# Windowed attention of a hybrid encoder step: three loop turns replaced by one unrolled pipeline of 36 items of two heads

## The chip, the core and the metric

The kernel runs on one core of a Trainium2 chip. The metric is the device time of one execution, in microseconds (us); lower is better. The core has engines that run in parallel and wait for each other through semaphores: PE (TensorE, matrix products and transposes; its weight loads are listed apart as PEld), DVE (VectorE), ACT (ScalarE), POOL (GpSimd), and SP, whose queue issues transfers. SBUF is the on-chip memory and PSUM the eight banks that PE writes to.

## The reference, cut to what matters

Two layers of an encoder, for a prompt of 512 tokens and a sample of 64. Only the windowed attention of layer 0 is touched by the change: 24 query heads of width 64, three key/value heads (8 query heads share one), chunks of 64 queries that see 192 keys, a linear distance bias and a sink per head.

```python
s = jnp.einsum('bcqkgd,bcskd->bckgqs', qb, kb).astype(jnp.float32) / math.sqrt(HEAD_DIM)
bias = -alibi_slopes()[:, :, None, None] * jnp.abs(dist).astype(jnp.float32)
s = jnp.where(valid, s + bias[None, None], -jnp.inf)
# sink_probs:
m = jnp.maximum(jnp.max(scores, axis=-1, keepdims=True), sink)
p = jnp.exp(scores - m)
p = p / (jnp.sum(p, axis=-1, keepdims=True) + jnp.exp(sink - m))
o = jnp.einsum('bckgqs,bcskd->bcqkgd', p.astype(v.dtype), vb)
```

The sample's 64 queries do the same over 128 cached keys and their own 64. Before this stand the projections of queries, keys and values; behind it a cross attention into 256 memory tokens, the output projection, a feed-forward block, and then the second layer.

## The kernel before

All data are fp32. A projection is a product of a weight slab (128 output channels, 1024 inputs) with all 576 tokens. Each fp32 operand is split in a high and a low part, so that a slab takes eight **eighths** of six matmuls each (`eighth`, L841: w_hi with hi, w_lo with hi, w_hi with lo, each in two halves of 288 tokens). ACT splits off `w_hi` (L440), POOL computes `w_lo` (L1788), SP loads the next slab.

The attention is worked through in 12 **query tiles** of two heads each (128 channels), four tiles (`QT`) for each key/value head. A tile has five **units** (`UNITS_J`): unit 0 is the sample's part of both heads; units 1 and 2 are the first head's two halves of the prompt, units 3 and 4 the second head's. A half with the prompt's start ("small") has 128 + 256 score columns and three 128x128 blocks; the other ("big") has 256 + 256 and four. Each unit goes through a chain over three engines:

- **S** (`scores`, L920 and L929): PE writes scores into one of two PSUM banks;
- **B** (`bias_max`, L1392 and L1399): DVE adds the bias into `prob` (four buffers) and takes the maximum;
- **E** (`exps`, L548 to L555): ACT takes the exponential, its sums and the sink's term;
- **N** (`norm`, L1407 to L1413): DVE adds, takes the reciprocal and scales `prob`;
- **T** (`transposes`, L941 to L946): PE transposes the blocks into bank 6;
- **C** (`copy_t`, L566 to L570): ACT copies them to `p_t` (two buffers);
- **V** (`values`, L959, L960, L967): PE multiplies with the values into bank 7; after units 0 and 4 DVE copies the result out (**O**, L1293).

The order of these steps is a list written by `attention_steps`, and every engine takes its own steps from the list, in that order: S of unit t stands beside T of unit t-3 and V of unit t-4 (`LAG_T`, `LAG_PV`). Between them stand 32 eighths (**K**) of projections for later query tiles, four slabs per turn. When a slab's eighths are done, DVE turns the result into the next query tile (**Q**, `query_tile`, L1365 and L1367) and ACT splits the slab after next. The list holds 20 units, and each engine runs it three times in a loop over the key/value heads (`Fori(0, KVH)`). At the start of a turn DVE copies that head's keys, values and sinks to `k_cur`, `v_s`, `v_cur` and `sink_cur`, and PE's first S waits for that (`cur_ready`). Because semaphore values in a loop depend on the turn, engines compute them in registers. `alone` puts the waits ahead of B on an instruction of their own.

## Time and profile before

| | |
|---|---|
| time, median of 3 executions | 1993.61 us (1992.95 to 1995.2) |
| span of the profiled execution | 1990.5 us (the median lies 3.1 us above it) |
| PE busy | 1862.8 us, 94% |
| DVE busy | 844.8 us, 42% |
| ACT busy | 634.1 us, 32% |
| POOL busy | 844.5 us, 42% |
| DMA | 145.16 MB, mean 73 GB/s |

The span runs from the first instruction of the program to the last. A timeline row gives a start, a duration, the engine and line, and how many records were merged in it (x6). PE's records overlap, since matmuls are pipelined: what one group costs PE is the difference between its start and the start of the next group. An fp32 matmul of the attention has two records, one for each pass; a transpose has one. "Chain" is the work followed back from the end: what released what. PEclk is the granted clock of TensorE, 1.00 for 2.4 GHz and 0.50 for 1.2 GHz.

### The profile page before, as it was taken

What the parts mean: (1) busy time and instruction counts of PE and PEld (TensorE: products, weight loads), DVE (VectorE), ACT (ScalarE), POOL (GpSimd) and SP (SyncE); (2) the same over time, 40 slices, a digit from 0 to 9 for tenths busy, and PEclk for the clock granted to TensorE, in tenths of its full rate; (3) what the DMA queues carried; (4) which work ended last, traced back from release to release, by engine and by line L of the source; (5) the groups of instructions that cost most, each with busy time, mean ns of one, the idle gap of its engine ahead of it and who ended that gap; (6) DMA issues with size and microseconds to landing.
All of it is one profiled execution on the core that took longest, in us unless ns stands there. A gap on an engine that the chain in (4) does not pass through costs nothing.

```text
span 1990.5 us, 33561 instructions
## 1 busy us (share of the span) xinstructions
PE 1862.8 (94%) x13089; PEld 1746.9 (88%) x13089; DVE 844.8 (42%) x1609; ACT 634.1 (32%) x1118; POOL 844.5 (42%) x510
## 2 busy tenths in 40 slices
PE   6999999898999999997998989899898899999995
PEld 6987777798899999996997878787798899999995
DVE  6346666612511111125867686764711611111124
ACT  6225545522312221223333324242622312222121
POOL 1221111134645444445456464746134644444453
PEclk9999999999899999997999999999999799999997
DMA  6521111022122222221221212121022122222221
GB/s 207 185 80 48 32 47 47 28 85 74 54 82 78 84 84 84 75 84 54 65 64 41 75 42 65 42 72 55 30 85 84 43 85 78 82 84 84 81 78 69
DMA packets 42161, 145.16 MB, mean 73 GB/s; under 512 B 4832, under 2 KB 6496, under 8 KB 41824
## 3 DMA queue, kind: packets, MB, share of 16 engines
q1 hardware_dynamic: 40288, 140.07, 23.3%
q10 hardware_dynamic: 1792, 3.97, 0.5%
q8 instruction: 56, 0.92, 0.2%
q14 instruction: 25, 0.20, 0.0%
HBM read 137.61 MB, written 6.41 MB: 72 GB/s over the span
## 4 chain that ended last, share of the span: by engine, by line
PE 80%; DVE 10%; issue 4%; ACT 3%; POOL 2%; DMA 0%; DVEq 0%; ACTq 0%; SPq 0%; POOLq 0%
PE ps L841 66%; PE ps L929 2%; PE ps L967 2%; DVE u L1617 2%; DVE mix L1300 2%; PE ps L946 1%; DVE mix L1264 1%; PE ps L1163 1%; PE ps L1029 1%; PE ps L1006 1%; DVE big_lo L1247 1%; PE ps L812 1%; POOL x L1807 1%; DVE mix L1744 1%; PE ps L1215 1%
## 5 line engine op out<-in xcount | busy, mean ns | idle before, releaser
L1788 POOL TENSOR_TENSOR w_lo<-raw,w_hi 128x1024 fp32r<-128x1024 f32 x228 | 562.3, 2466 | 1026.5 <-ACT w_hi L440 1023.9
L841 PE MATMUL ps<-big_hi,w_hi 128*128 128x288 f32 x3616 | 804.4, 304 | 22.8 <-ACT big_hi L464 15.8
L841 PE MATMUL ps<-big_lo,w_hi 128*128 128x288 f32 x3616 | 786.9, 300 | 13.3 <-DVE big_lo L1247 13.1
L841 PE MATMUL ps<-big_hi,w_lo 128*128 128x288 f32 x3616 | 785.1, 299 | 0.0
L841 PEld LDWEIGHTS ps<-big_hi,w_hi 128*128 128x128 f32 x3616 | 590.0, 191 | 37.2 <-issue 30.8
L841 PEld LDWEIGHTS ps<-big_lo,w_hi 128*128 128x128 f32 x3616 | 590.4, 191 | 20.8 <-DVE big_lo L1247 20.6
L841 PEld LDWEIGHTS ps<-big_hi,w_lo 128*128 128x128 f32 x3616 | 592.2, 191 | 0.0
L440 ACT ACTIVATE w_hi<-raw 128x1024 fp32r<-128x1024 f32 x242 | 256.3, 1059 | 799.2 <-PE ps L841 782.1
L1539 DVE TENSOR_TENSOR mix<-ps,mix 128x576 f32<-128x576 f32 x64 | 48.4, 757 | 315.9 <-PE ps L841 315.9
L1527 DVE SCALAR_TENSOR_TENSOR relu<-ps,rstd 128x576 f32<-128x576 f32 x64 | 48.5, 757 | 311.6 <-PE ps L841 305.6
L1617 DVE SCALAR_TENSOR_TENSOR u<-xp,cpar,u 128x579 f32<-128x579 f32 x84 | 88.0, 1047 | 6.8 <-ACT u L703 4.8
L1282 DVE TENSOR_TENSOR sq_sum<-sq_sum,sq 128x576 f32<-128x576 f32 x24 | 19.9, 828 | 136.8 <-ACT sq L453 136.7
L1823 POOL TENSOR_TENSOR hid<-relu 128x576 f32<-128x576 f32 x64 | 73.5, 1148 | 8.5 <-DVE relu L1527 8.5
L1807 POOL TENSOR_TENSOR x<-x,mix 128x576 f32<-128x576 f32 x29 | 55.3, 1920 | 34.2 <-DVE mix L1300 18.0
L1392 DVE CUSTOM_DVE_ANT_0 prob<-ps,bias,sink_cur 128x128 f32<-128x128 f32 (+2 forms) x120 | 49.4, 442 | 37.1 <-PE ps L929 35.1
L548 ACT ACTIVATE prob<-prob,stat 128x256 f32<-128x256 f32 (+2 forms) x108 | 50.9, 472 | 41.6 <-DVE stat L1399 40.8
L1245 DVE TENSOR_TENSOR big_lo<-hid,big_hi 128x576 fp32r<-128x576 f32 x64 | 48.1, 751 | 28.4 <-POOL hid L1823 28.4
L1293 DVE TENSOR_SCALAR mix<-ps 64x64 f32 (+5 forms) x72 | 35.8, 497 | 52.5 <-PE ps L967 29.2
L841 PE MATMUL ps<-m_hi,w_hi 128*128 128x256 f32 x128 | 39.0, 305 | 15.4 <-POOL w_lo L1788 11.4
L759 ACT ACTIVATE dec<-ps 128x384 f32<-128x384 f32 (+1 forms) x40 | 16.1, 454 | 107.9 <-PE ps L1163 107.9
L929 PE MATMUL ps<-k_cur,q_t 64*128 64x128 f32 (+1 forms) x192 | 49.5, 378 | 0.0
L1707 DVE TENSOR_TENSOR dec<-dec,cbm 128x768 f32<-128x768 f32 (+1 forms) x20 | 26.7, 1337 | 48.3 <-ACT dec L759 48.3
(190 smaller groups left out, 1760.7 us busy)
## 6 DMA issues: line engine op xcount, KB each, us to landing
raw<-in_slabs SPq DMA_DIRECT2D x242, 512.0 KB, 3.6
bias<-in_alibi SPq DMA_DIRECT2D x14, 256.0 KB, 2.6
x<-in_x SPq DMA_DIRECT2D x2, 1152.0 KB, 6.6
out_y<-x SPq DMA_DIRECT2D x3, 576.0 KB, 2.8
out_h<-state ACTq DMA_DIRECT2D x4, 384.0 KB, 2.4
out_mv<-vm ACTq DMA_DIRECT2D x2, 512.0 KB, 5.8
kms<-in_mk SPq DMA_DIRECT2D x2, 512.0 KB, 5.4
vms<-in_mv SPq DMA_DIRECT2D x2, 512.0 KB, 7.0
```

The source lines that it names most:

```text
L440: act.activation(w_hi[:, s % 2], raw[:, s % 2], ACT.Copy).then_inc(hi_done, 1)
L548: act.activation(ap, ap, ACT.Exp, bias=stat[:, r, 1, b:b + 1], accum_out=stat[:, r, 2, b:b + 1])
L841: ins = pe.matmul(ps[:, 2 * (g % 2) + h, 0:hi_c - lo_c], w[:, s % 2, kt], a[:, k0 + kt, lo_c:hi_c], start=(start and kt == 0 and w is w_hi ...
L929: ins = pe.matmul(ps[:, bank, b * 2 * P + c:(b + 1) * 2 * P], q_t[e * HD:(e + 1) * HD, j, DEC + i * P:DEC + (i + 1) * P], k_cur[e * HD:(e ...
L1245: ins = dve.tensor_tensor(dst, src, hi.bitcast(F32), ALU.subtract)
L1392: ins = dve.tensor_tensor_reduce(prob[half, r, k, c0:c1], ps[half, bank, k * 2 * P + c0:k * 2 * P + c1], bias[half, j % 2, e, c0 + d:c1 + ...
L1527: dve.scalar_tensor_tensor(out=halves(relu[:, m % 2]), in0=src, scalar=0.0, in1=halves(rstd[:, 1]), op0=ALU.max, op1=ALU.mult).then_inc(fr ...
L1539: dve.tensor_tensor(halves(mix[:, m]), src, halves(mix[:, m]), ALU.add).then_inc(freed, 1)
L1617: dve.scalar_tensor_tensor(out=u[:, t], in0=xp[:, t % 2, j:j + UC], scalar=cpar[:, t, j:j + 1], in1=u[:, t], op0=ALU.mult, op1=ALU.add).th ...
L1788: pool.tensor_tensor(w_lo[:, s % 2], raw[:, s % 2], w_hi[:, s % 2].bitcast(F32), ALU.subtract).then_inc(lo_done, 1)
L1807: pool.tensor_tensor(x[:, m], x[:, m], mix[:, m], ALU.add).then_inc(x_done, 1)
L1823: pool.tensor_tensor(hid[:, m % 2], relu[:, m % 2], relu[:, m % 2], ALU.mult).then_inc(hid_done, 1)
```

## The change

The three turns become one straight list without a loop, over all 60 units, and with it go the copies to `k_cur`, `v_s`, `v_cur` and `sink_cur` (the products read `k_all`, `v_all` and `par`), the register arithmetic and `alone`. Units are renumbered: 1 and 2 are now the small halves of both heads, 3 and 4 the big ones. PE works in 36 **items** (`WORKS`), three for each tile: the sample, the two small halves, the two big halves. `scores` of a pair alternates matmul by matmul between the heads, that is between rows 0 to 63 and 64 to 127 of the array and between the two score banks. `values` of a pair alternates between columns 0 to 63 and 64 to 127, in one bank. The sample's values are four matmuls of 64 columns in place of two of 128, and one copy takes them out in place of two.

The list has 38 slots. Slot w holds S of item w, B of its units, V of item w-2, eighths, and then for each unit in turn E of item w and N and T of item w-1, with eighths between; O comes last. The 96 eighths are spread evenly, two or three in a slot.

```diff
+def work_units(w):
+    t = w // 3 * UNITS_J
+    return (t,) if w % 3 == 0 else (t + 2 * (w % 3) - 1, t + 2 * (w % 3))
 def attention_steps():
-    steps, k, total = [], 0, UNITS + LAG_PV
-    for t in range(total):
-        if t < UNITS:
-            steps.append(("S", t))
-        if 0 <= t - LAG_T < UNITS:
-            steps.append(("T", t - LAG_T))
-        while k < QT * KT and (k - 1) * (total - 1) <= t * QT * KT and k + 1 < KT * (1 + (t + 1) // UNITS_J):
-            steps.append(("K", k))
-            k += 1
-        if 0 <= t - LAG_PV < UNITS:
-            steps.append(("V", t - LAG_PV))
+    for w in range(slots):
+        goal = TILES * KT * (w + 1) // slots
+        new = work_units(w) if w < WORKS else ()
+        old = work_units(w - 1) if 0 <= w - 1 < WORKS else ()
+        if new:
+            steps.append(("S", w))
+        steps += [("B", t) for t in new]
+        if w >= 2:
+            steps.append(("V", w - 2))
+        fill(goal - 1 if len(old) > 1 else goal)
+        for c in range(2):
+            steps += [("E", t) for t in new[c:c + 1]]
+            steps += [(kind, t) for t in old[c:c + 1] for kind in "NT"]
+            if c < len(old):
+                fill(goal)
+        if w >= 2:
+            steps.append(("O", w - 2))
...
+                pe.wait_ge(biased, n_)
+                for b in range(2):
...
+                    for e in range(2):
+                        ins = pe.matmul(ps[:, S_BANK + (t + e) % 2, b * 2 * P + c:(b + 1) * 2 * P],
                                         q_t[e * HD:(e + 1) * HD, j, DEC + i * P:DEC + (i + 1) * P],
-                                        k_cur[e * HD:(e + 1) * HD, keys[0]:keys[1]], start=True, stop=True)
+                                        k_all[e * HD:(e + 1) * HD, g, keys[0]:keys[1]], start=True, stop=True)
...
+                def product(e, rows, v, a, b, p0, start):
+                    return pe.matmul(ps[e * HD:(e + 1) * HD, O_BANK, a:b], v_all[0:rows, v, g],
+                                     p_t[0:rows, (n_ + (e if u else 0)) % 2, p0:p0 + b - a], start=start, stop=True,
+                                     skip_group_check=True)
...
+                for k, (v, a, b, p0, start) in enumerate(parts):
+                    for e in range(2):
+                        ins = product(e, P, v, a, b, p0, start)
...
-                copy(k_cur[:], k_g)
-                for e in range(2):
-                    copy(v_s[:, 0, e], v_g[:, 0])
-                    copy(v_s[0:DEC, 1, e], v_g[0:DEC, 1])
-                copy(v_cur[:, 2:], v_g[:, 2:])
-                copy(sink_cur[:], par[:, bass.ds(g * GROUP + C_SINK, GROUP)]).then_inc(cur_ready, 1)
+            for kind, t in STEPS:
+                if kind == "B":
+                    bias_max(t)
+                elif kind == "N":
+                    norm(t)
+                elif kind == "O":
+                    take_out(t)
+                elif kind == "K" and t % KT == KT - 1:
+                    s = t // KT
+                    query_tile(s, q_t[:, s % QT], q_s[:, s % QT] if s < TILES - QT else None)
```

PE before, in the middle of a turn (L929 is S, L946 T, L841 an eighth, L967 V):

```order
L967 MATMUL ps<-p_t,v_cur 64x256 [waits o_done]
L967 MATMUL ps<-p_t,v_cur 64x128
L916 REGISTER_ALU
L929 MATMUL ps<-k_cur,q_t 128x128 [waits biased]
L929 MATMUL ps<-k_cur,q_t 128x256
L946 MATMUL ps<-mats,prob 128x128 [waits pt_done,normed]
L946 MATMUL ps<-mats,prob 128x128 x2
```

PE after, the slot of a tile's big halves (L932 is S, L961 V of the sample, L950 T, L841 an eighth):

```order
L932 MATMUL ps<-k_all,q_t 128x256 [waits biased]
L932 MATMUL ps<-k_all,q_t 128x256 x3
L961 MATMUL ps<-p_t,v_all 64x64 [waits o_done,pt_done]
L961 MATMUL ps<-p_t,v_all 64x64 x3
L841 MATMUL ps<-big_hi,w_hi 128x288 x2
L841 MATMUL ps<-big_hi,w_lo 128x288 x2
L841 MATMUL ps<-big_lo,w_hi 128x288 x2
L950 MATMUL ps<-mats,prob 128x128 [waits pt_done,normed]
L950 MATMUL ps<-mats,prob 128x128 x2
```

S and V now take two heads at once, and T, which before took up a unit whose S lay three units back, takes up the item of the slot just before.

DVE before, where a slab's query tile is made (L1392 is B, L1407 to L1413 N, L1365 and L1367 Q):

```order
L1399 TENSOR_SCALAR stat<-stat 128x1 [waits biased]
L1407 TENSOR_TENSOR stat<-stat 128x2 [waits exp_done]
L385 REGISTER_ALU
L1409 RECIPROCAL stat<-stat 128x2 [waits dve_self]
L385 REGISTER_ALU
L1413 TENSOR_SCALAR prob<-prob,stat 128x256 [waits dve_self]
L1413 TENSOR_SCALAR prob<-prob,stat 128x256
L1287 REGISTER_ALU
L1365 SCALAR_TENSOR_TENSOR q_s<-ps,rstd 64x64 [waits slab_done]
L1365 SCALAR_TENSOR_TENSOR q_s<-ps,rstd 64x64
L1367 SCALAR_TENSOR_TENSOR q_t<-ps,rstd 128x576
```

DVE after, in slot 3 (L1405 ends B, L1372 and L1374 are Q, L1413 to L1419 N):

```order
L1405 TENSOR_SCALAR stat<-stat 128x1 [waits biased]
L1372 SCALAR_TENSOR_TENSOR q_s<-ps,rstd 64x64 [waits slab_done]
L1372 SCALAR_TENSOR_TENSOR q_s<-ps,rstd 64x64
L1374 SCALAR_TENSOR_TENSOR q_t<-ps,rstd 128x576
L1413 TENSOR_TENSOR stat<-stat 128x2 [waits exp_done]
L1415 RECIPROCAL stat<-stat 128x2 [waits dve_self]
L1419 TENSOR_SCALAR prob<-prob,stat 128x256 [waits dve_self]
L1419 TENSOR_SCALAR prob<-prob,stat 128x256
```

Q, with its wait for a slab, now stands ahead of the N that follows B.

## Rows read from the trace of the kernel before

**Rows 1.** The timeline of all engines: first score, second turn, end of the attention (start, duration, work)

```profile
134.15 0.49 PE L920 MATMUL ps<-k_cur,q_s 128*128 128x192 f32 x2
...
206.90 0.59 PE L920 MATMUL ps<-k_cur,q_s 128*128 128x192 f32 x2 [3.05 <-DVE sink_cur L1293]
...
351.78 0.75 DVE L1367 SCALAR_TENSOR_TENSOR q_t<-ps,rstd 128x576 f32<-128x576 f32 x1
352.63 0.62 PE L1006 MATMUL ps<-kms,q_t 128*64 128x256 f32 x2 [1.60 <-issue]
```

**Rows 2.** The waits from 134 to 352 us (total, times, longest)

```profile
PE ps L920 <- DVE sink_cur L1293: 6.1, 2, 3.0
```

**Rows 3.** PE's timeline through one big and one small unit, and a sample's unit

```profile
162.39 0.59 PE L920 MATMUL ps<-k_cur,q_s 128*128 128x192 f32 x2
162.82 0.60 PE L946 MATMUL ps<-mats,prob 128*128 128x128 f32 x4
...
167.87 1.08 PE L967 MATMUL ps<-p_t,v_cur 128*64 128x128 f32 x6
168.88 1.13 PE L929 MATMUL ps<-k_cur,q_t 64*128 64x256 f32 x4
169.94 0.66 PE L946 MATMUL ps<-mats,prob 128*128 128x128 f32 x4
170.35 0.51 PE L841 MATMUL ps<-big_hi,w_hi 128*128 128x288 f32 x2
...
171.33 0.86 PE L967 MATMUL ps<-p_t,v_cur 128*64 128x256 f32 x4
172.12 0.92 PE L929 MATMUL ps<-k_cur,q_t 64*128 64x128 f32 x4
172.97 0.33 PE L941 MATMUL ps<-mats,prob 128*128 128x128 f32 x1
```

**Rows 4.** The chain of waits, one of its pieces (start, duration, what)

```profile
166.34 1.60 PE ps L841 x12
```

**Rows 5.** PE's timeline in layer 1: six matmuls that alternate between column halves

```profile
1042.16 0.88 PE L1193 MATMUL ps<-dec,sq 128*64 128x128 f32 x12
1042.97 0.53 PE L841 MATMUL ps<-big_hi,w_hi 128*128 128x288 f32 x2
```

**Rows 6.** DVE's timeline: B and N of several units, and a Q

```profile
177.29 0.48 DVE L1392 CUSTOM_DVE_ANT_0 prob<-ps,bias,sink_cur 128x256 f32<-128x256 f32 x1 [0.44 <-PE ps L929]
...
178.30 0.15 DVE L1407 TENSOR_TENSOR stat<-stat 128x2 f32<-128x2 f32 x1
...
179.74 0.41 DVE L1392 CUSTOM_DVE_ANT_0 prob<-ps,bias,sink_cur 64x192 f32<-64x192 f32 x1
...
180.71 0.15 DVE L1407 TENSOR_TENSOR stat<-stat 128x2 f32<-128x2 f32 x1
...
181.09 0.61 DVE L1413 TENSOR_SCALAR prob<-prob,stat 128x256 f32<-128x256 f32 x2
182.61 0.35 DVE L1392 CUSTOM_DVE_ANT_0 prob<-ps,bias,sink_cur 128x128 f32<-128x128 f32 x1 [0.91 <-PE ps L929]
...
183.49 0.15 DVE L1407 TENSOR_TENSOR stat<-stat 128x1 f32<-128x1 f32 x1
...
184.51 0.46 DVE L1365 SCALAR_TENSOR_TENSOR q_s<-ps,rstd 64x64 f32<-64x64 f32 x2 [0.32 <-PE ps L841]
```

**Rows 7.** ACT's timeline: an E and a C of a big unit

```profile
178.43 0.51 ACT L548 ACTIVATE prob<-prob,stat 128x256 f32<-128x256 f32 x1 [0.34 <-DVE stat L1399]
...
179.43 0.28 ACT L555 ACTIVATE stat<-stat,sink_cur 128x2 f32<-128x2 f32 x1
179.99 0.60 ACT L570 ACTIVATE p_t<-ps 128x512 f32<-128x512 f32 x1 [0.28 <-PE ps L946]
```

**Rows 8.** Busy time by stretch: us, PE, PEld, DVE, ACT, POOL, PEclk, DMA, GB/s

```profile
134.00:207.00 73.00, 69.95 (x428) 54.90 (x427) 48.34 (x208) 38.93 (x125) 11.83 (x5) 1.00 0.15 49
...
280.00:284.00 4.00, 4.00 (x18) 3.60 (x17) 1.87 (x7) 1.02 (x4) 0.00 (x0) 0.57 0.00 0
```

More of the change, by code:

```diff
@@ L544, in exps @@
                 else:
-                    e = (u - 1) // 2
-                    parts = [(b, prob[:, r, b, P if u % 2 and b == 0 else 0:2 * P]) for b in range(2)]
+                    parts = [(b, prob[:, r, b, P if u < 3 and b == 0 else 0:2 * P]) for b in range(2)]
                 for b, ap in parts:
@@ L943, in transposes @@
                 else:
-                    tiles = [(0, 1), (1, 0), (1, 1)] if u % 2 else [(0, 0), (0, 1), (1, 0), (1, 1)]
+                    tiles = [(0, 1), (1, 0), (1, 1)] if u < 3 else [(0, 0), (0, 1), (1, 0), (1, 1)]
                     for k, (b, key) in enumerate(tiles):
@@ L976, in values @@
-                ins.then_inc(v_done, 1)
-            loop.per = ATT_PER
-            with pe.Fori(0, KVH) as g:
-                loop.i = g
-                for kind, t in STEPS:
-                    if kind == "S":
-                        scores(t)
-                    elif kind == "T":
-                        transposes(t)
-                    elif kind == "V":
-                        values(t)
-                    else:
-                        if t % KT == 0:
-                            begin(n.s + t // KT, n.g + t // KT)
-                        eighth(n.s + t // KT, n.g + t // KT, t % KT, big_hi, big_lo, KT)
-                loop.i = None
@@ new lines, in _ @@
+            pe.wait_ge(cache_in, 32)
+            pe.wait_ge(va_done, BLOCKS)
+            for kind, t in STEPS:
+                if kind == "S":
+                    scores(t)
+                elif kind == "T":
+                    transposes(t)
+                elif kind == "V":
+                    values(t)
+                elif kind == "K":
+                    if t % KT == 0:
+                        begin(n.s + t // KT, n.g + t // KT)
+                    eighth(n.s + t // KT, n.g + t // KT, t % KT, big_hi, big_lo, KT)
@@ L1459, in _, with take_out @@
-            own.n += (KVH - 1) * ATT_PER["dve_self"]
-            n.s += KVH * QT
-            n.g += KVH * QT
-            n.n += KVH * UNITS
-            query_tile(QT - 1, q_t[:, QT - 1])
-            for i in range(2):
-                dve.wait_ge(bias_in[i], 16 * (KVH * QT // 2 + 1))
+                    normalise(n.n + t, P, [(0, P if u < 3 else 0, 2 * P), (1, 0, 2 * P)])
+            def take_out(w):
+                t, q = work_units(w)[-1], w // 3
+                if w % 3 == 1:
+                    return
+                dve.wait_ge(v_done, n.n + t + 1)
+                if w % 3:
+                    copy(mix[:, q, DEC:TOK], ps[:, O_BANK]).then_inc(o_done, 1)
+                else:
+                    copy(mix[:, q, 0:DEC], ps[:, O_BANK, 0:DEC]).then_inc(o_done, 1)
```

227 lines of the change are left out of this document (86 added, 141 removed).

## The prediction

> **What bounds the kernel now.** I read the page first: PE is busy 94% of the span, so only what stands on PE, or what makes PE wait, can count. Then the timeline gives the place: the attention lasts from the first score at 134.15 to the first score of the cross attention at 352.63, 218.5 us [rows 1]; nothing else is changed. The busy time by stretch shows PE busy for 70 of the 73 us of the first turn, DVE for 48 and ACT for 39 [rows 8]. The waits tell where PE stood still: 6.1 us in two waits, at the start of turns 2 and 3, for DVE's copies [rows 1, 2].
>
> PE's cost by step is the difference of starts [rows 3]: V big 1.01, S big 1.06, T big 0.41, an eighth with a switch on both sides 0.98, V small 0.79, S small 0.85, S of the sample 0.43. Two eighths in a row take 1.60, so one takes 0.80 [rows 4]. A tile has eight eighths (6.4), S 2 x (0.85 + 1.06) = 3.8, V 2 x (0.79 + 1.01) = 3.6, four T and the sample's (three quarters of 0.41 for a small one) 1.6, the sample's S and V about 1.1, and some ten switches of 0.09: 17.4. Four tiles are 70, with the 3 us stall 73, as measured. So PE alone bounds this stretch; the lags of three and four units hide the chain over DVE and ACT.
>
> **What the change takes from PE.** For the column halves this trace has the same form: six matmuls of 128 columns, 12 passes, take 0.81 us [rows 5]; 0.11 a pass one after another would be 1.3. They run in pairs, so V of two heads should cost what one head's did, 0.79 and 1.01. For the row halves no row shows it. If they pair too, S of both heads costs 0.85 and 1.06; if not, twice that. I take the first, since both heads then load other rows and write other banks. The saving is 1.9 + 1.8 = 3.7 us a tile, 44 in 12 tiles, with some 3 for the sample's values and 6.1 for the turns: about 53. PE's own work falls from 17.4 to 13.4 a tile.
>
> The Trainium skill ("TensorEngine Tiling (Array Packing)", Key Properties) says that different tiles of the array load and multiply in parallel, row tiles too, and its Gotcha 1 that row tiles must not share a bank. By that rule the first case holds for S; no row here shows it. The same section says that a change of tiling mode drains the engine; the trace agrees, with the 0.09 us of a switch.
>
> **What takes PE's place.** T now belongs to the item of the slot before, and its N stands on DVE behind B of this slot, which waits for S of this slot. DVE's steps are [rows 6]: B big 1.01 (177.29 to 178.30), B small 0.88, B of the sample 0.97, N big 0.99 to its end (180.71 to 181.70), N small, with 128 columns fewer, about 0.94, N of the sample about 0.7 (one scaling in place of two), Q 1.23 (two of 0.23 and 0.76), 0.75 in the last four, which have no sample [rows 1]. ACT's are E big 1.28 and C big 0.60 [rows 7]. I follow a tile slot by slot from PE's start of S:
>
> - *Big slot.* DVE starts at 1.2 (S's record ends at 1.13), two B to 3.2, the first N to 4.15, and T of the first unit at 4.3. PE is through with S, V of the sample (0.5) and one or two eighths by 2.5 or 3.3: it stands. Then T 0.3, an eighth 0.88, T 0.33: the slot takes 5.8, and the number of eighths doesn't matter.
> - *Sample slot.* S 0.43. V of the small pair needs C of its second unit, which on ACT stands behind C of the first and an E of 1.2: ready at about 1.3. V 0.79, an eighth 0.90 and in half the slots another: T of the first big unit at 3.0 or 3.8. The next T must wait for C of the first: 0.41 + 0.27 + 0.60 + 0.1 = 1.4 later, then 0.5. 4.9 with two eighths, 5.7 with three.
> - *Small slot.* S 0.85, V big 1.05, two eighths 1.70 or three 2.50, T of the sample with the switch 0.36: 4.0 or 4.8. DVE has that N ready at 3.6, so PE is the bound here.
>
> By the list there are 12 big slots (69.6), sample slots with three eighths six times and with two five times (58.7), small slots with three five times and two six times (48.0); the first two slots take 5.9. That is 182.2 us.
>
> To this comes Q. It stands on DVE at the eighth that ends a slab, and DVE waits there for PE. In slots 3, 6 and 9 it stands ahead of both N: PE ends the slab at 3.1 (slot 9: 3.9), Q ends 1.23 later, N 0.99, then T, where it would have come at 3.8 or 3.0: 1.7, 2.5 and 2.5 us. In slots 12, 15 and 18 it stands between the two N: 2.4 each. In the small slots 22, 25, 28, 31, 34 it holds up the sample's N: 0.6, 1.4, 1.0, 1.8, 1.8. Sum 20.5. ACT's split of the next slab waits for the same eighth; I take it that it ends before Q does, with nothing behind it that is late. The last two slots have no S, one V each and six eighths, and end with Q and its 0.75: 11.1 (before, too, the first cross score waited for that Q, at 351.78).
>
> Sum: 182.2 + 20.5 + 11.1 = 213.8 against 218.5: 4.7 us less. So of 53 us taken from PE, all but 5 come back as waits in the slots. The profiled span would be 1985.8, and the median, which lies 3.1 above it, **1988.9 us**.
>
> What costs nothing: DVE's copies are already counted as PE's two stalls; register arithmetic and `alone` lie in the sequencers; SP's loads for a slab are issued four slots before ACT takes it up, and the bias tables three slots ahead. The unit's chain has no other use of POOL. Bounds: each hand-over that I set at 0.1 may be 0 or 0.2; with four or five on the path of a slot, of 38 slots, that is 15 us either way at the extreme, and about 6 as I take it. For S the upper end is the serial one, below.
>
> **Rivals.**
>
> 1. *The row halves don't pair.* S costs 1.06 more in 12 big slots, where DVE waits for it, and 0.85 in 12 small ones, where PE is the bound: 22.9 more, 2012. For it: all S rows of before stay in one half for a unit, so nothing contradicts it. Against it: the column halves pair [rows 5]. 7%.
> 2. *The clock falls in the new stalls (the slower side).* Where PE had stood for 3 us, at the start of the third turn [rows 2], the granted clock fell: 0.57 in 280 to 284 [rows 8], that is 1.2 GHz for 3.4 us, about 1.7 us lost; before the second turn the same stall had no such effect [rows 1]. The new waits are shorter, up to 2.5 us in the Q slots and 1 to 1.8 in the others. If each of the 11 Q slots and a few big ones brought it down, 12 us or more would be lost: 2001. It decides from about 6 falls on, and I see none or one. 13%. The Trainium skill ("TensorE: Matmul & The Clock Gate", Part 1) has the clock drop after an idle window; one of the two long stalls here agrees.
> 3. *The waits are much shorter than my slots say*, because hand-overs are short and Q's waits overlap with others: a big slot of 5.3, a sample slot of 5.0, Q at 12: 218.5 less 22, 1972. 17%.
> 4. *PE stays the bound*, and the change does all that it frees: 218.5 less 53, 1941. Against it: in the big slot B, B and N are 3 us in a row that no reorder hides. 3%.
> 5. *The unrolled code costs*: instruction loading holds engines up, and eats the 5 us: 1995. Against it: I see no reason why straight code should run slower than the loop's, whose pace is in [rows 4], so 7%.
>
> **How the numbers follow.** The forecast has 53%; its own range is 1981 to 1997. A measurement here can tell a change from about 0.2%, 4 us. Faster by more than that: a bit over half of the forecast's share (0.31), rivals 3 and 4: 0.51. Slower: rivals 1 and 2 (0.17 of 0.20) and the upper tail of the forecast (0.06): 0.23. The same: 0.26. For 8 in 10 the range leaves out rivals 1 and 4 and the far ends: 1970 to 2003.
>
> **What the profile after would show.** V and S pairs: a merged row of eight S passes with about 1.06 to the next start is right, 2.1 would be rival 1. PE busy in the attention down to about 165 of 214 us. T (L950) waiting for DVE's N (L1419) in every third slot, 1 to 1.8 us; V (L961) waiting for ACT's C in sample slots, about 0.8; 11 waits of DVE's Q (L1372, L1374) for L841. The stretch from first S to first cross score 214 us. The prediction is wrong if PE's waits for `normed` in the big slots are under half a microsecond, if Q's slots are no longer than the others, or if the clock in the stretch is below 0.97.

## The result, and the profile after

The changed kernel takes **2014.39 us** (median of 4 runs, 2013.25 to 2015.49); the kernel before took 1993.71 in the same comparison (1992.95 to 1995.2). The ratio is 1.0089, with a 95% interval of 1.0062 to 1.0116: it is slower by about 0.9%. The forecast was 1988.9 with a range of 1970 to 2003. The profiled execution has a span of 2011.5 us, 21.0 more than before.

In every comparison below, "the stretch" is the time from the first score of the attention to the first score of the cross attention: 134.15 to 352.63 before [rows 1], 218.5 us; 134.25 to 373.24 after, 239.0 us. Behind it both profiles need the same time to the end (1637.9 us before, 1638.2 after, and between 1636 and 1640 in all kernels here). So the loss lies in the stretch: it is 20.5 us longer than before, where 213.8 was forecast, 4.7 less than before.

The busy time from 134 to 374 us after (window, length, busy us and instructions of PE, PEld, DVE, ACT, POOL, then PEclk, DMA share, GB/s):

```profile
134.00:374.00 240.00, 187.43 (x1327) 148.75 (x1326) 141.71 (x584) 111.10 (x373) 28.72 (x13) 0.91 0.11 39
```

PE was busy for 70 of 73 us in a turn [rows 8]; now it is idle for a fifth of the time, and the granted clock, 1.00 in nearly all of the stretch before, is 0.91. Summed over the records, PE ran at 1.2 GHz for 44.4 us of the stretch, against 3.4 before. The waits in it (engine, tile and line, releaser: us in total, times, longest):

```profile
DVE prob L1398 <- PE ps L932: 50.7, 24, 3.5
PE ps L950 <- DVE prob L1419: 35.8, 17, 4.0
DVE q_s L1372 <- PE ps L841: 16.7, 7, 5.2
DVE prob L1398 <- PE ps L921: 16.1, 11, 2.7
PE ps L945 <- DVE prob L1419: 8.7, 5, 2.9
PE ps L961 <- ACT p_t L578: 7.0, 11, 0.9
```

PE now stands 44.5 us for DVE's scaling at the end of N (L1419: 35.8 + 8.7); before, it stood for none of this, only 6.1 us for the copies [rows 2]. DVE stands 67 us for scores (50.7 + 16.1). They take turns: that much was forecast. What PE does when it runs at full clock is as cheap as forecast. PE's timeline of the changed kernel (start, us, engine, line, form, records merged):

```profile
267.84 1.13 PE L932 MATMUL ps<-k_all,q_t 64*128 64x256 f32 x8
268.90 0.60 PE L961 MATMUL ps<-p_t,v_all 128*64 128x64 f32 x8
...
253.88 0.87 PE L961 MATMUL ps<-p_t,v_all 128*64 128x256 f32 x8 [0.60 <-ACT p_t L578]
...
254.68 0.53 PE L841 MATMUL ps<-big_hi,w_hi 128*128 128x288 f32 x2
```

S big of two heads takes 1.06 to the next start (267.84 to 268.90), which one head took before [rows 3], and V small of two heads 0.80.

So why 25 us more than forecast? One slot shows it. This is slot 18, around a Q (all engines, in order of time):

```profile
257.81 0.46 DVE L1372 SCALAR_TENSOR_TENSOR q_s<-ps,rstd 64x64 f32<-64x64 f32 x2 [2.52 <-PE ps L841]
257.87 1.06 ACT L450 ACTIVATE w_hi<-raw 128x1024 fp32r<-128x1024 f32 x1 [0.26 <-PE ps L841]
258.28 0.76 DVE L1374 SCALAR_TENSOR_TENSOR q_t<-ps,rstd 128x576 f32<-128x576 f32 x1
...
259.01 2.34 POOL L1772 TENSOR_TENSOR w_lo<-raw,w_hi 128x1024 fp32r<-128x1024 f32 x1 [19.76 <-ACT w_hi L450]
259.14 0.17 DVE L1415 RECIPROCAL stat<-stat 128x2 f32<-128x2 f32 x1
259.34 2.41 DVE L1419 TENSOR_SCALAR prob<-prob,stat 128x256 f32<-128x256 f32 x2
261.81 0.42 PEld L950 LDWEIGHTS ps<-mats,prob 128*128 128x128 f32 x4 [4.27 <-DVE prob L1419]
261.81 0.66 PE L950 MATMUL ps<-mats,prob 128*128 128x128 f32 x4 [4.04 <-DVE prob L1419]
```

The last eighth of a slab releases three things at once: DVE's Q at 257.81, ACT's split at 257.87 and, through the split, POOL's subtraction (`w_lo`, L1772) at 259.01. N stands right behind Q on DVE, and its two scalings, 0.61 together at another time [rows 6], take 2.41 here. POOL ends at 259.01 + 2.34 = 261.35, and only then the first scaling ends and the second runs. The reciprocal beside it (259.14, 0.17) isn't held up. PE stood for 4.04 us. In slot 22, a small one, the sample's single scaling (0.32 when free) meets the same:

```profile
282.54 2.35 POOL L1772 TENSOR_TENSOR w_lo<-raw,w_hi 128x1024 fp32r<-128x1024 f32 x1 [21.19 <-ACT w_hi L450]
...
282.87 2.13 DVE L1419 TENSOR_SCALAR prob<-prob,stat 128x192 f32<-128x192 f32 x1
...
285.06 0.33 PE L945 MATMUL ps<-mats,prob 128*128 128x128 f32 x1 [2.16 <-DVE prob L1419]
```

And after such a stall the clock falls. PE alone, around slot 18 (length, busy, PEclk, DMA share, GB/s):

```profile
252.00:258.00 6.00, 5.18 (x40) 1.00 0.26 98
258.00:262.30 4.30, 0.49 (x4) 1.00 0.00 0
262.30:263.00 0.70, 0.70 (x10) 0.98 0.00 0
263.00:266.40 3.40, 3.40 (x20) 0.50 0.01 2
266.40:270.00 3.60, 3.60 (x32) 1.00 0.00 0
```

PE was busy for 0.49 of 4.3 us; 1.2 us after it resumes at 261.81 it goes to 1.2 GHz for 3.4 us, and V big, which starts in it, takes 1.90 us to the next start (263.47 to 265.37) where it takes 1.02 at full clock. There are nine such places in the stretch, four of them with 6.8 us instead of 3.4. Eight of them follow the eight stalls in which POOL held a scaling up (2.2 to 4.0 us long), the ninth follows a stall of 1.6 us; other stalls of 1.6 us had no such effect.

So two things look likely: the block by POOL, and the clock that falls behind the longer stalls. The experiments take them apart.

### The profile page after: what moved, and what is told of

Its sections match the earlier page's. It is cut to its first block, busy times and chain, and to the rows that moved or that the text cites. A ratio compares the mean times of both kernels' runs of the same rounds, so it can differ in the third digit from the quotient of the medians.

```text
span 2011.5 us, 33114 instructions
## 1 busy us (share of the span) xinstructions
PE 1837.3 (91%) x13137; PEld 1728.4 (86%) x13137; DVE 839.3 (42%) x1570; ACT 630.4 (31%) x1118; POOL 844.0 (42%) x510
## 3 DMA queue, kind: packets, MB, share of 16 engines
q1 hardware_dynamic: 40000, 139.55, 20.5%
## 4 chain that ended last, share of the span: by engine, by line
PE 73%; DVE 12%; issue 7%; ACT 4%; POOL 3%; DMA 1%; ACTq 0%; DVEq 0%; SPq 0%; POOLq 0%
PE ps L841 63%; DVE u L1601 2%; DVE mix L1307 2%; PE ps L932 1%; PE ps L961 1%; DVE mix L1271 1%; PE ps L950 1%; DVE prob L1419 1%; PE ps L1170 1%; DVE prob L1398 1%; DMA raw<-in_slabs 1%; DVE big_lo L1254 1%; ACT w_hi L450 1%; POOL x L1791 1%; DVE mix L1728 1%
## 5 line engine op out<-in xcount | busy, mean ns | idle before, releaser
L1772 POOL TENSOR_TENSOR w_lo<-raw,w_hi 128x1024 fp32r<-128x1024 f32 x228 | 561.8, 2464 | 1048.9 <-ACT w_hi L450 1040.6
L841 PE MATMUL ps<-big_hi,w_hi 128*128 128x288 f32 x3616 | 806.7, 305 | 23.2 <-ACT big_hi L474 15.8
L841 PE MATMUL ps<-big_lo,w_hi 128*128 128x288 f32 x3616 | 789.5, 300 | 13.3 <-DVE big_lo L1254 13.0
L841 PE MATMUL ps<-big_hi,w_lo 128*128 128x288 f32 x3616 | 787.5, 300 | 0.0
L841 PEld LDWEIGHTS ps<-big_hi,w_hi 128*128 128x128 f32 x3616 | 591.7, 192 | 41.5 <-issue 33.5
L841 PEld LDWEIGHTS ps<-big_lo,w_hi 128*128 128x128 f32 x3616 | 592.6, 192 | 21.0 <-DVE big_lo L1254 20.8
L841 PEld LDWEIGHTS ps<-big_hi,w_lo 128*128 128x128 f32 x3616 | 594.1, 192 | 0.0
L1398 DVE CUSTOM_DVE_ANT_0 prob<-ps,bias,par 128x128 f32<-128x128 f32 (+2 forms) x120 | 49.5, 442 | 67.0 <-PE ps L932 50.7
L950 PE MATMUL ps<-mats,prob 128*128 128x128 f32 x168 | 31.4, 310 | 35.8 <-DVE prob L1419 35.8
L1419 DVE TENSOR_SCALAR prob<-prob,stat 128x256 f32<-128x256 f32 (+3 forms) x148 | 58.8, 434 | 3.0
L950 PEld LDWEIGHTS ps<-mats,prob 128*128 128x128 f32 x168 | 21.1, 155 | 41.9 <-DVE prob L1419 39.9
L841 PE MATMUL ps<-m_hi,w_hi 128*128 128x256 f32 x128 | 38.5, 301 | 15.3 <-ACT m_hi L496 11.0
L759 ACT ACTIVATE dec<-ps 128x384 f32<-128x384 f32 (+1 forms) x40 | 16.1, 454 | 107.9 <-PE ps L1170 107.9
```

The source lines that it names most:

```text
L841: ins = pe.matmul(ps[:, 2 * (g % 2) + h, 0:hi_c - lo_c], w[:, s % 2, kt], a[:, k0 + kt, lo_c:hi_c], start=(start and kt == 0 and w is w_hi ...
L950: ins = pe.transpose(ps[:, T_BANK, k * P:(k + 1) * P], prob[:, r, b, key * P:(key + 1) * P], mats[:, 0])
L1398: ins = dve.tensor_tensor_reduce(prob[half, r, k, c0:c1], ps[half, bank, k * 2 * P + c0:k * 2 * P + c1], bias[half, j, e, c0 + d:c1 + d], 1.0,
L1419: ins = dve.tensor_scalar(ap, ap, stat[0:rows, r, 2, b:b + 1], None, ALU.mult)
L1772: pool.tensor_tensor(w_lo[:, s % 2], raw[:, s % 2], w_hi[:, s % 2].bitcast(F32), ALU.subtract).then_inc(lo_done, 1)
```

## The experiments

Each kernel was timed beside the kernel before on the same chip. The first two rows are of one comparison. In the others the kernel before had medians of 1994.6 to 1999.2 us, not 1993.7, so times of different rows can be compared to a few us only; the ratio is the safer number. The stretch is read from one profile of each kernel. The table has them together (stretch: from its profile; half clock: us of the stretch at 1.2 GHz, summed over the records; ratio to before with its 95% interval).

| kernel | time, us | ratio | stretch | half clock |
|---|---|---|---|---|
| before | 1993.7 | | 218.5 | 3.4 |
| after | 2014.39 | 1.0089 (1.0062 to 1.0116) | 239.0 | 44.4 |
| e_nolow | 1989.78 | 0.9962 (0.9939 to 0.9986) | 215.6 | 13.7 |
| e_chunk | 1993.38 | 0.9984 (0.9966 to 1.0001) | 218.5 | 20.5 |
| e_filler | 2000.99 | 1.0021 (1.0006 to 1.0035) | 226.1 | 3.4 |
| e_late | 1985.93 | 0.9940 (0.9923 to 0.9957) | 212.6 | 23.9 |
| e_late_chunk | 1970.95 | 0.9877 (0.9855 to 0.9898) | 195.6 | 3.4 |
| e_nfirst | 1960.09 | 0.9807 (0.9789 to 0.9824) | 184.8 | 10.2 |
| e_best | 1944.65 | 0.9735 (0.9698 to 0.9772) | 168.6 | 0 |
| e_serial | 2017.82 | 1.0100 (1.0079 to 1.0120) | 242.2 | 44.4 |
| e_best_serial | 1946.03 | 0.9751 (0.9731 to 0.9771) | 171.9 | 0 |
| e_best_apart | 1981.31 | 0.9919 (0.9898 to 0.9940) | 207.4 | 0 |
| e_unroll | 1992.14 | 0.9980 (0.9964 to 0.9997) | 209.9 | 4.8 |
| e_unroll_chunk | 1991.56 | 0.9980 (0.9965 to 0.9994) | 209.9 | 4.8 |

### Is it POOL's subtraction? (e_nolow, e_chunk)

In e_nolow the subtraction of the attention's slabs is cut to one column, and POOL's wait for the slab before goes with it. So this kernel leaves out the low part of 12 slabs, which a real kernel needs:

```diff
-            slabs_lo(TILES)
+            for k in range(TILES):
...
+                pool.tensor_tensor(w_lo[:, s % 2, 0, 0:1], raw[:, s % 2, 0, 0:1], w_hi[:, s % 2, 0, 0:1].bitcast(F32), ALU.subtract).then_inc(lo_done, 1)
```

> Leaves out the low part of the 12 weight slabs used inside the attention: POOL subtracts one column in place of 1024, all else as in the changed kernel. Theory A (DVE's scaling in N, which ran 1.0 to 2.2 us in place of 0.32 to 0.35 wherever POOL's 2.4 us subtraction ran beside it, 14.4 us in sum, is the larger part of the miss, and the stalls it stretches bring the clock down): the scaling keeps 0.32 to 0.35 us everywhere, the stretch from the first score to the first cross score falls from 239 us to 214 to 220, the half clock in it from 44 us to under 15; time about 1991. Rival B (the clock falls by itself once PE stands 2 us or more, the subtraction only happens to lie there): at most the 14 us go, the half clock stays near 44 us, time 2000 to 2003. Rival C (the long scaling is covered by other waits): 2012 to 2014.

Measured: 1989.78, stretch 215.6, 23.4 less than the changed kernel and 1.8 from the forecast's 213.8 (with 13.7 us at half clock in it, of which the forecast had none; more on that below). The scaling's rows of the two kernels (busy us, mean ns | idle before), first of the changed one, then of e_nolow:

```profile
L1419 DVE TENSOR_SCALAR prob<-prob,stat 128x256 f32<-128x256 f32 x72 | 33.9, 498 | 0.8
...
L1419 DVE TENSOR_SCALAR prob<-prob,stat 128x192 f32<-128x192 f32 x12 | 7.5, 621 | 0.4
```

```profile
L1419 DVE TENSOR_SCALAR prob<-prob,stat 128x256 f32<-128x256 f32 x72 | 23.1, 350 | 0.8
...
L1419 DVE TENSOR_SCALAR prob<-prob,stat 128x192 f32<-128x192 f32 x12 | 3.8, 320 | 0.4
```

14.5 us of the scaling were waiting on POOL ((33.9 - 23.1) + (7.5 - 3.8)): eight of these 84 operations take 2.12 to 2.15 us each, the others 0.32 to 0.36. Slot 18 of e_nolow shows what one block costs (PE alone):

```profile
239.86 0.49 PE L921 MATMUL ps<-k_all,q_s 128*128 128x192 f32 x2
...
247.09 0.66 PE L950 MATMUL ps<-mats,prob 128*128 128x128 f32 x4 [2.24 <-DVE prob L1419]
247.68 0.93 PE L932 MATMUL ps<-k_all,q_t 64*128 64x128 f32 x8
```

and the same slot of the changed kernel:

```profile
252.79 0.49 PE L921 MATMUL ps<-k_all,q_s 128*128 128x192 f32 x2
...
262.40 0.38 PE L932 MATMUL ps<-k_all,q_t 64*128 64x128 f32 x2
```

Both are at full clock. The slot takes 7.82 without the block and 9.61 with it, 1.79 more, and PE's stall is 2.24 instead of 4.04.

e_chunk keeps the work and only cuts it into pieces, one for each of the eight input groups:

```diff
-            slabs_lo(TILES)
+            for k in range(TILES):
...
+                for kt in range(KT):
+                    ins = pool.tensor_tensor(w_lo[:, s % 2, kt], raw[:, s % 2, kt], w_hi[:, s % 2, kt].bitcast(F32), ALU.subtract)
+                ins.then_inc(lo_done, 1)
```

> The changed kernel, whole, with POOL's subtraction of each attention slab cut into eight pieces of 128 columns. If DVE's scaling is blocked for as long as one POOL instruction lasts, it now waits 0.3 to 0.4 us in place of up to 2.1: the 14.4 us of long scalings become 3 to 5, the half clock in the stretch falls from 44 us to 10 to 25, and the time comes near that of the kernel without the low part, 1989 to 1995. Rival (the two engines share a bandwidth, and the same bytes cost the same): the long scalings stay, 2010 to 2014.

Measured: 1993.38, stretch 218.5, as expected: 20.5 less than the changed kernel for an edit that gives POOL more to do. The rival, that the two engines share a bandwidth, is out. The scaling and POOL in it:

```profile
L1419 DVE TENSOR_SCALAR prob<-prob,stat 128x256 f32<-128x256 f32 x72 | 24.9, 375 | 0.8
```

```profile
L1844 POOL TENSOR_TENSOR w_lo<-raw,w_hi 128x128 fp32r<-128x128 f32 x88 | 38.1, 468 | 161.8 <-ACT w_hi L450 161.8
```

The block acts like a lock held for a whole instruction: a piece of 0.47 us holds a scaling up by 0.2 at most, the whole one of 2.34 by 1.8. In pieces it reaches other operations too: N's sum (`TENSOR_TENSOR` on two columns, 0.15 when free) takes up to 0.41 here. The blocked time of all of DVE's operations is 3.3 us in e_chunk. The Trainium skill ("SBUF — State Buffer", "Who interferes with whom") says this of the port pair that VectorE and GpSimd share: whoever starts first has it for its whole instruction, and `tensor_scalar` is among the operations that can need it. The traces agree, in the 2.41 us above.

### How much of it is the clock? (e_filler)

e_filler keeps the blocked scaling, and lets PE do 26 more matmuls in eight slots, ahead of the T that waits. They write to the columns of a projection bank that the sums don't use; the kernel's results are wrong with them all the same, and why wasn't looked into. It is a probe of time alone:

```diff
+FILLED = ((3, 0), (6, 0), (9, 0), (12, 1), (15, 1), (18, 1), (22, 0), (25, 0))
...
+            if (w, c) in FILLED:
+                steps.append(("F", w))
...
+                    for _ in range(26):
+                        pe.matmul(ps[:, 2 * (g1 % 2), HALF:512], big_hi[:, KT, 0:P], big_hi[:, KT, 0:512 - HALF], start=True, stop=True,
+                                  skip_group_check=True)
```

> The changed kernel with 26 more matmuls (2.5 us, their result is not used) in the eight slots where PE stood longest (3, 6, 9, 12, 15, 18, 22, 25), just ahead of the transposes that wait. It prices the clock alone: if the clock falls because PE stands in those slots, the half clock in the stretch goes from 44 us to under 15, and the stretch from 239 us to 226 to 232, time 2001 to 2008, though more work is done. Rival (the falls have another cause, or cost nothing because PE isn't the bound in the slots behind them): 2013 to 2016. If the filler is longer than the stall somewhere, that costs up to 1 us a slot.

Measured: 2000.99, stretch 226.1, 3.4 us at half clock instead of 44.4, and the scaling still blocked:

```profile
L1428 DVE TENSOR_SCALAR prob<-prob,stat 128x256 f32<-128x256 f32 x72 | 34.2, 503 | 0.8
```

```profile
134.00:360.00 226.00, 194.19 (x1537) 160.39 (x1537) 140.75 (x581) 109.89 (x372) 28.63 (x12) 0.99 0.12 43
```

So giving PE more work made the kernel 13 us faster: 239.0 - 226.1 = 12.9 is what the clock cost at least, since a filler may take a little time of its own and one fall is left. The rest of the gap to the forecast, 226.1 - 213.8 = 12.3, is less than the block's 8 x 1.8 = 14.4, because the forecast was too long elsewhere (see the slots below). The two aren't independent: the block makes the stalls longer behind which the clock falls. But it isn't their only cause. In e_nolow no stall is longer than 2.25 us, and the clock still falls four times, once behind a stall of 1.56; in e_chunk it falls six times, with no stall over 2.44.

### The order on DVE (e_late, e_late_chunk, e_nfirst, e_best)

e_late puts Q and the split that goes with it at the slot's end, behind both N:

```diff
+        while ended < k // KT:
+            steps.append(("Q", ended))
+            ended += 1
...
-                elif kind == "K" and t % KT == KT - 1:
+                elif kind == "Q":
```

> Only the place of the query tile on DVE (Q) and of the next slab's split on ACT is changed: they stand at the end of the slot in which a slab ends, not at the eighth that ends it, so DVE no longer waits for PE ahead of N, and POOL's subtraction starts later. Theory A (waits of Q for PE and the collision of N with POOL are what made the Q slots 9 to 11 us long): Q slots fall to 5 to 6.5 us, the collision moves to DVE's small operation after B with at most 1.3 us each, the stretch becomes about 205 us, time about 1980. Rival B (the clock falls with any stall of 1 to 2 us and costs what it did): stretch about 215 to 220, time 1990 to 1995. Rival C (the long slots come from the order of N behind B alone): no change, 2010 to 2014.

Measured: 1985.93, stretch 212.6, 26.4 less, but 8 more than theory A had. Q no longer holds N up, but POOL's subtraction moved with it and now meets B of the next slot:

```profile
L1408 DVE TENSOR_SCALAR stat<-stat 128x2 f32<-128x2 f32 x48 | 24.9, 519 | 1.7
```

This is an operation on two columns, 0.17 us when it is free. One of them, at 258.66, takes 1.84. The blocked time is 16.8 us, more than in the changed kernel, and the stretch is shorter even so; how much of it is hidden by DVE's waits for PE wasn't taken apart. The clock still falls, for 23.9 us. With POOL in pieces:

> The changed kernel with Q and the split at the slot's end and POOL's subtraction in eight pieces: of the four things that made its slots long (Q's wait for PE, the block by POOL, the clock, N behind B) only the last is left. By the slots of the forecast without Q's term, 182 + 11 us: stretch 190 to 196, half clock under 8 us, time 1965 to 1972. Against the kernel with N ahead of B and all else the same (168.6 us) that prices the order alone at 22 to 27 us. Rival (the block and Q were all): stretch 170 to 175.

Measured: 1970.95, stretch 195.6. The forecast's slots without the Q terms make 182.2 + 11.1 = 193.3, so the slot model is right within 2.3 us once the two things that it lacked are gone. In part that is luck: the plain slots took 190.2 (see below), and Q at a slot's end made some slots behind it longer (the big ones from slot 23 on by 0.9 us and more), which makes about 5.4 in all, with the one fall of the clock. The bound in the model is real: B, B and N in a row. e_nfirst takes that away, with N and T of a unit ahead of B and E. Q and the split stand at the slot's end, as in e_late, and no eighth stands ahead of the first T any more, where the changed kernel had one or two (in small slots two or three):

```diff
-        steps += [("B", t) for t in new]
...
-        fill(goal - 1 if len(old) > 1 else goal)
         for c in range(2):
-            steps += [("E", t) for t in new[c:c + 1]]
             steps += [(kind, t) for t in old[c:c + 1] for kind in "NT"]
-            if c < len(old):
-                fill(goal)
+            if c == 0:
+                fill(goal - 1)
+            steps += [(kind, t) for t in new[c:c + 1] for kind in "BE"]
+        fill(goal)
```

> The changed kernel with another order in the slot: for each unit in turn N and T of the item before, then B and E of the new item; one eighth less ahead of the first T; Q and the slab's split at the slot's end. Nothing else is changed. Theory A (the slot's length was set by S, B, B, N, T in a row, because N stood behind B of the same slot): T is ready right after V, PE is the bound again with 13.4 us a tile, less about 2 us where POOL's subtraction blocks DVE: stretch 165 to 185 us, half clock under 10 us, time 1940 to 1960. Rival (chain through E and C on ACT is as long): stretch 200 or more, time 1975 or more.

Measured: 1960.09, stretch 184.8, at the upper end of theory A. e_best is this with POOL's subtraction in eight pieces:

> The order with N ahead of B (as in the run before), with POOL's subtraction in eight pieces. The slots in which POOL blocked DVE (5.8 to 7.6 us in place of 4.7) go back to about 4.9: stretch 185 to 168 to 174, time 1944 to 1950 where that order alone had 1960. Rival (those slots were long for Q, not for the block): 1958 to 1960.

Measured: **1944.65**, 2.65% faster than before, the lowest time of all. Stretch 168.6, no half clock:

```profile
134.00:303.00 169.00, 162.68 (x1326) 134.31 (x1324) 131.11 (x583) 110.43 (x373) 40.43 (x89) 1.00 0.17 55
```

PE is busy for 96% of it again. Against e_late_chunk, the order in the slot alone (N and T ahead of B and E, the eighths behind T) is worth 27.0 us of the stretch. POOL's 3.42 us in pieces lie across DVE's work here, and the operation that waited 1.84 in e_late takes 0.47:

```profile
190.78 3.42 POOL L1846 TENSOR_TENSOR w_lo<-raw,w_hi 128x128 fp32r<-128x128 f32 x8 [9.40 <-ACT w_hi L452]
...
191.05 0.32 DVE L1421 TENSOR_SCALAR prob<-prob,stat 128x192 f32<-128x192 f32 x1
...
192.07 0.47 DVE L1407 TENSOR_SCALAR stat<-stat 128x2 f32<-128x2 f32 x1
```

### Is alternating needed? (e_serial, e_best_serial, e_best_apart)

e_serial issues S and V of a pair one head after the other:

```diff
-                for b in range(2):
...
-                    for e in range(2):
+                for e in range(2):
+                    for b in range(2):
...
-                for k, (v, a, b, p0, start) in enumerate(parts):
-                    for e in range(2):
+                for e in range(2):
+                    for k, (v, a, b, p0, start) in enumerate(parts):
```

> The changed kernel with the same matmuls in another order: scores and values of a pair do all of the first head, then all of the second, so that neighbouring matmuls stay in the same half of the array. Theory A (alternating halves run in pairs, which the records 5 to 7 ns apart say): S and V take twice as long; small slots grow by 0.85 + 1.0 us, sample slots by 0.8, big slots by nothing, since there DVE is the bound and the first head's scores are ready sooner: about 30 us more, 2040 to 2047. Rival (my first reckoning, that S delays B by its whole length in big slots too): 12 x 1.06 more on top, about 2055. Rival (the pairs are only a matter of how records are stamped): 2014.

Measured: 2017.82, stretch 242.2, only 3.2 more where some 30 were expected. DVE bounds the changed kernel, which could have hidden the rest, so the same edit was tried on e_best, where PE is the bound.

> The kernel with N ahead of B and the subtraction in pieces, but with the scores and values of a pair one head after the other, so that the halves of the array do not alternate. There PE is the bound (164 of 171 us busy), so the doubling of S and V should count in full: 12 x (1.91 + 1.80) = 44 us, less a few where the first head's scores are ready sooner: stretch 205 to 213, time 1982 to 1990; in the changed kernel the same edit cost only 3 to 4 us. Rival (the pairing is worth little anywhere): 1945 to 1950.

Measured: 1946.03, stretch 171.9, 3.3 more where 44 were expected: what the expectation's rival said. PE's timeline of e_best_serial shows why:

```profile
195.87 1.14 PE L934 MATMUL ps<-k_all,q_t 64*128 64x256 f32 x8
196.94 0.60 PE L963 MATMUL ps<-p_t,v_all 128*64 128x64 f32 x8
...
191.82 1.36 PE L963 MATMUL ps<-p_t,v_all 128*64 128x128 f32 x12
193.11 0.33 PE L947 MATMUL ps<-mats,prob 128*128 128x128 f32 x1
```

and e_best, with the heads alternating:

```profile
177.72 1.09 PE L963 MATMUL ps<-p_t,v_all 128*64 128x128 f32 x12
178.74 0.33 PE L947 MATMUL ps<-mats,prob 128*128 128x128 f32 x1
```

S big still takes 1.07 for both heads. Its eight records start in pairs, at 195.874 and 195.887, 196.194 and 196.207, and so on; in e_best the two of a pair start 7 ns apart, here 13 ns. The first head has four passes ahead of the second's first here and two there, at about 3.3 ns each. That fits passes that are issued in order, quickly, and then wait for their own half of the array, but no run tests that reading by itself. V big, six passes of a head, takes 1.29 instead of 1.02: the second head's first pass starts at 192.095, with the third of the first head (192.089), so some of the overlap is lost when six passes of one half stand ahead of the other. With four, in S big, S small and V small, 0.01 us is lost (V small takes 0.81 instead of 0.80). Twelve times 0.27 is 3.2, nearly the whole difference of the two stretches.

The edit had thus hardly undone the pairing. e_best_apart does: it puts work of another tiling between the two heads.

```diff
+                elif kind == "S":
+                    for e in range(2):
+                        if t % 3:
+                            scores(t, (e,))
+                        elif e:
+                            scores(t)
+                        if (t - 2) % 3:
+                            values(t - 2, (e,))
+                        elif e == 0:
+                            values(t - 2)
```

> The kernel of e_best (N and T of a unit ahead of B and E, Q at the end of the slot, POOL's subtraction in eight pieces), with one thing changed on TensorE alone: the passes of the two heads of a pair stand apart. A slot issues S of the first head, V of the first, S of the second, V of the second (where one of them is the sample's, it stands whole between the two heads of the other), so between two heads' scores there is always work of another tiling. Only the last two slots keep V of both heads together. Theory A (what the change brings to TensorE is that two heads' passes overlap in the two halves, and the matmul-by-matmul alternation is not needed, since e_best_serial lost only 3 us of the stretch): each head costs alone what the pair did, so PE has 12 x (0.85 + 1.06) for S and 11 x (0.79 + 1.01) for V more, 42.7 us, and some 36 changes of tiling at 0.09, 3 us. PE was busy for 164 of 169 us in e_best, so nearly all of it shows: stretch 212 to 216 instead of 168.6, ratio to before about 0.997, time about 1990. Theory B (VectorE would bound the stretch at nearly the same length, and the pairing is of little use): stretch 180 to 190, ratio 0.982. Theory C (heads in different halves overlap across another tiling's work too, as they did in the serial order): stretch under 175, ratio 0.975 to 0.978.

Measured: 1981.31, stretch 207.4: 38.9 more than e_best, and 5 to 9 less than expected. PE's timeline and its busy time:

```profile
192.06 1.13 PE L935 MATMUL ps<-k_all,q_t 64*128 64x256 f32 x4
193.12 0.60 PE L964 MATMUL ps<-p_t,v_all 128*64 128x64 f32 x8
193.65 1.13 PE L935 MATMUL ps<-k_all,q_t 64*128 64x256 f32 x4
194.70 0.55 PE L953 MATMUL ps<-mats,prob 128*128 128x128 f32 x3
```

```profile
134.00:345.00 211.00, 206.94 (x1334) 161.61 (x1334) 136.78 (x588) 109.70 (x375) 42.47 (x96) 1.00 0.14 46
```

Each head alone takes 1.05 or 1.06, as before. PE's more work was sized right: busy time in the stretch is 204.2 against 162.1, 42.1 more for the 42.7 expected. But 3.2 us of it filled waits that e_best still had (6.4 us there, 3.2 here), and the changes of tiling between S and V, put at 3 us, cost nothing that shows (S small takes 0.85 to the start of V, as before). So the pairing is real, and worth 39 us of the stretch where PE is the bound.

### The loop (e_unroll, e_unroll_chunk)

e_unroll is the kernel before with its list written out straight: no loop, no copies per turn, same order of steps.

```diff
-                copy(k_cur[:], k_g)
...
+                    copy(v_s[:, g, 0, e], v_all[:, 0, g])
...
-            with pe.Fori(0, KVH) as g:
...
+            for kind, t in STEPS:
```

> The kernel before, with its own order of steps and its own products, but one straight list of 60 units: no turns, no copies of keys and values between them. Theory: what the changed kernel gained by this part alone is PE's two stalls of 3.05 us and the 3.4 us of half clock behind one of them, about 8 us: stretch 210 to 212, 1986 to 1989 where the kernel before has 1993.6 to 1997.9. Rival (the list's end effects cost as much): no change.

Measured: 1992.14, ratio 0.998, where 1986 to 1989 was expected; the stretch is 8.6 shorter, as expected, but starts 7.2 later, since all twelve copies to `v_s` stand ahead of it. They are 0.18 us each, and the second of them meets POOL's subtraction and takes 2.33:

```profile
137.88 3.45 DVE L1281 TENSOR_SCALAR v_s<-v_all 128x64 f32<-128x64 f32 x12
137.92 2.34 POOL L1757 TENSOR_TENSOR w_lo<-raw,w_hi 128x1024 fp32r<-128x1024 f32 x1 [4.00 <-ACT w_hi L438]
141.38 0.50 PEld L912 LDWEIGHTS ps<-k_all,q_s 128*128 128x128 f32 x2 [4.93 <-DVE v_s L1281]
```

> The kernel before, unrolled, with POOL's subtraction of the attention slabs in eight pieces. There DVE was blocked too (9 of its small operations after B took 0.92 us on average in place of 0.17), but PE was the bound and had transposes three units in hand: no change, stretch 209 to 211, 1989 to 1993. Rival (the block cost there as well): 5 us less or more.

Measured: 1991.56, 0.6 us from e_unroll, within what the runs tell apart. The stretch starts 2.6 earlier (138.79), and has the same length, 209.9, though the two-column operation behind B takes 0.19 us in the mean instead of 0.37. So in this order, with transposes in hand for PE, the block costs the stretch nothing: it was there in the kernel before, under cover. This row is of the kernel before; an operation of 0.17 has a mean of 0.311, for nine of the 48 ran beside POOL's subtraction and took 0.92 in the mean:

```profile
L1399 DVE TENSOR_SCALAR stat<-stat 128x2 f32<-128x2 f32 x48 | 14.9, 311 | 1.7
```

## Why the prediction was wrong, point by point

**The step that failed** is the one on Q: "ACT's split of the next slab waits for the same eighth; I take it that it ends before Q does, with nothing behind it that is late", and further down "The unit's chain has no other use of POOL". The split does end about when Q does, but what it releases is POOL's subtraction, which locks DVE's scaling out for 1.8 us just when PE waits for it: a term of eight times 1.8, 14.4 us, that the sum had at nothing. In the kernel before the same collision showed in plain rows, in a mean of 311 ns for a two-column operation that takes 170 when free, and the prediction didn't ask why.

**The second step that failed** is on the clock (rival 2, 13%): "I see none or one". There were nine places with a fall, and they came at the price that the rival named: "12 us or more would be lost: 2001", measured 12.9 (e_filler). The block lengthened the stalls to 4 us and so brought on most of the falls, but "none or one" would have been wrong without it too: e_nolow has stalls of 1.6 to 2.25 us, none longer than the forecast's own 2.5, and four falls. The two together, less some 4 us by which the rest of the sum was too long, are the 25.2 us by which the stretch missed. Neither alone would have left the range: 2014.4 less the cost of either is about 2000.

**The slots** were nearly right. A plain slot, without Q and at full clock, takes 5.80 if it is big (forecast 5.8), 4.73 or 5.53 if it is a sample's (4.9 or 5.7), 3.89 or, in e_late_chunk, 4.69 if it is small (4.0 or 4.8); the first two take 6.1 together (5.9) and the last two 10.9 (11.1). With the numbers of slots of the forecast that is 190.2 instead of 193.3. That N behind B takes PE's place as the bound is shown by e_best, which only turns the order in the slot round against e_late_chunk and gains 27.

**Q's own wait** was put at 20.5 us over eleven slots, and was right. In e_nolow, where nothing is blocked, nine of these slots are free of the clock's fall. Read from PE's timeline, from S to S, they are longer than a plain slot of their kind by 1.67 (slot 3), 2.46 (9), 2.29 (12 and 18), 0.57 (22), 1.36 (25), 0.89 (28) and 1.69 (31 and 34): 14.9 us, where the forecast had 15.6 for these nine.

So the forecast was some 4 us too long in what it did count. Without the block and at full clock this order would take about 210 us (190.2 and some 19.7 for Q), not 213.8; the block's 14.4 and some 14 or 15 for the clock make the 239.0. It follows that e_nolow's 215.6 came so near to the forecast partly by luck: it holds some 6 us for the clock that the forecast didn't have.

**The pairing (rival 1, 7%)** was called right: S of both heads costs 1.06, not 2.1. That it needs the alternation was never tested by the prediction, and it doesn't, within the groups of up to four passes here.

**Rival 3** (shorter waits) fell: the slots and Q came out 3.9 us shorter in sum, not 22. **Rival 4** (PE stays the bound, 1941) fell for this order of steps, but was right on what could be freed: e_best takes 1944.65. What the prediction held against it, that B, B and N are "3 us in a row that no reorder hides", was wrong: e_nfirst and e_best hide them, by moving N ahead of B. **Rival 5** (unrolled code costs) fell: e_unroll is not slower.

The signs that the prediction named did their work: it said that it would be wrong if the clock in the stretch is below 0.97, and it is 0.91. The 11 waits of Q for L841 (7 and 4) and the waits of V for ACT's C (11 times, up to 0.9) were there as named.

**What stays open.** The block and the clock can't be priced wholly apart, since the block causes part of the stalls behind which the clock falls. Why one stall of 1.6 us is followed by a fall and the next isn't, no run here shows. Why e_unroll's stretch is 8.6 shorter than before's wasn't taken apart: 6.1 us are the copies' two waits [rows 2]; the time at half clock is no shorter (4.8 against 3.4), so the rest may be the loop itself.

## What to carry to other kernels

When a change takes work from the engine that bounds a pipeline, follow each semaphore that fires at the moment where the next engine becomes critical, on all engines, not only along the chain: here one release started DVE, ACT and, through ACT, POOL, and POOL then kept DVE out. An operation with a far larger mean than its neighbours of the same kind is a collision that something hides at present; look at it before removing the cover. A long GpSimd instruction beside critical VectorE work can be cut in pieces, and the work that another engine is waiting for belongs first in its engine's order.

## What the runs showed of the hardware

- POOL's fp32 subtraction of 128x1024 (2.34 us) holds up DVE's `TENSOR_SCALAR` on SBUF, one of 128x256 (0.35 free, 2.15 blocked) as well as one of 128x2 (0.17 free, 1.84 blocked in e_late), and not the reciprocal (0.17 beside it) nor B's operation that reads PSUM (0.48 with and without). In eight pieces it takes POOL 3.42 instead of 2.34, and the changed kernel gets 20.5 us of the stretch back.
- PE at 1.2 GHz for 3.4 us or twice that came after stalls of 1.6 to 4.0 us in this stretch, though not after every stall of 1.6. The fall began between 0.9 us before and 1.8 us after PE resumed, and always reached into the work behind the stall, so it is that work that pays. Matmuls without use in the stalls were worth 12.9 us.
- Passes of matmuls for different halves of the array overlap without being alternated: four passes of one half ahead of the other cost 0.01 us, six cost 0.27. With work of another tiling between them they don't overlap (1.05 for each head's S big).
